# Expert weights as plain float32 and token slots in column tiles of 32, in a diffusion-step kernel

## What is computed

```python
def _expert_choice_ffn(h, router_w, wg, wu, wd):
    cap = EC_CAPACITY_FACTOR * n // N_EXPERTS            # 64 latent, 16 context slots
    probs = jax.nn.softmax((h @ router_w).astype(jnp.float32), axis=-1)
    gate, idx = lax.top_k(jnp.swapaxes(probs, 1, 2), cap)
    xs = h[b_idx, idx]
    hid = jax.nn.silu(jnp.einsum('becd,edf->becf', xs, wg)) * jnp.einsum('becd,edf->becf', xs, wu)
    ye = jnp.einsum('becf,efd->becd', hid, wd) * gate[..., None]
    return jnp.zeros_like(h).at[b_idx, idx].add(ye)
```

## Time and profile before

| | us |
|---|---|
| median of 3 runs | 1666.2 (1665.37 to 1667.24) |
| the profiled execution, its own time | 1663.94 |
| its span, first to last instruction | 1662.1 |
| PE's first and last expert matmul in it | 497.6 to 1627.4 |

### The profile page before, as it was taken

One profiled execution on the slowest core, in us unless ns is written; L12 is line 12 of the kernel. 1 busy time (PEld: TensorE's weight loads), 2 busy tenths in 40 slices (PEclk: granted clock), 3 DMA queues, 4 the chain that ended last, 5 costly groups with the idle time before them and its releaser, 6 DMA issues.

```text
span 1662.1 us, 18848 instructions
## 1 busy us (share of the span) xinstructions
PE 1504.0 (90%) x6785; PEld 1002.2 (60%) x6785; DVE 1207.9 (73%) x1072; ACT 964.2 (58%) x832; POOL 146.5 (9%) x80
## 2 busy tenths in 40 slices
PE   5798898669929999999999999999999999999991
PEld 2586676538806666666666666666666666666660
DVE  2536635332477888888888888889888888888883
ACT  3323444211416677776777777767767677767762
POOL 0422311200000000000000000000000000000000
PEclk9799999869859999999999999999999999999996
DMA  9321112481179999999999999999999999999953
GB/s 363 112 77 51 51 64 62 169 295 63 59 268 359 341 383 358 366 370 358 384 361 364 371 356 390 353 378 352 367 377 354 380 356 368 380 346 389 356 236 134
DMA packets 124210, 478.77 MB, mean 288 GB/s; under 512 B 11534, under 2 KB 13834, under 8 KB 107788
## 3 DMA queue, kind: packets, MB, share of 16 engines
q1 hardware_dynamic: 113796, 453.55, 73.0%
q0 software_dynamic: 3072, 10.49, 2.6%
q10 hardware_dynamic: 7304, 14.23, 2.4%
HBM read 464.59 MB, written 13.64 MB: 288 GB/s over the span
## 4 chain that ended last, share of the span: by engine, by line
PE 51%; DVE 21%; issue 12%; ACT 10%; DMA 5%; ACTq 0%; POOL 0%; DVEq 0%; SPq 0%; POOLq 0%
DVE w_lo L311 11%; PE bank L1047 8%; PE bank L1043 8%; PE bank L1044 8%; ACT w_hi L305 6%; PE bank L1061 4%; PE bank L1057 4%; PE bank L1058 4%; PE bank L346 3%; PE bank L348 3%; PE bank L347 3%; DMA raw<-in_ada_w 2%; PE bank L748 1%; PE bank L1070 1%; DVE arena L1456 1%
## 5 line engine op out<-in xcount | busy, mean ns | idle before, releaser
L311 DVE TENSOR_TENSOR w_lo<-raw,w_hi 128x2048 fp32r<-128x2048 f32 (+1 forms) x211 | 476.0, 2263 | 177.1 <-ACT w_hi L305 177.1
L305 ACT CAST w_hi<-raw 128x2048 fp32r<-128x2048 f32 x211 | 400.1, 1910 | 205.6 <-PE bank L1047 67.9
L311 DVE TENSOR_TENSOR w_lo<-arena,w_hi 128x2048 fp32r<-128x2048 f32 x189 | 427.0, 2285 | 52.4 <-ACT w_hi L305 52.4
L1043 PE MATMUL bank<-w_hi,act_lo 128*80 128x512 f32 x1024 | 406.5, 397 | 2.6 <-DVE act_lo L1462 2.3
L305 ACT CAST w_hi<-arena 128x2048 fp32r<-128x2048 f32 x189 | 357.9, 1910 | 80.7 <-PE bank L1047 79.7
L1044 PE MATMUL bank<-w_hi,act_hi 128*80 128x512 f32 x1024 | 402.6, 393 | 0.0
L1047 PE MATMUL bank<-w_lo,act_hi 128*80 128x512 f32 x1024 | 280.6, 396 | 3.7 <-DVE w_lo L311 3.7
L1043 PEld LDWEIGHTS bank<-w_hi,act_lo 128*80 128x80 f32 x1024 | 153.5, 150 | 90.0 <-ACT w_hi L305 6.9
L1047 PEld LDWEIGHTS bank<-w_lo,act_hi 128*80 128x80 f32 x1024 | 150.6, 148 | 94.1 <-DVE w_lo L311 10.8
L1057 PE MATMUL bank<-w_hi,act_lo 128*80 128x512 f32 x512 | 203.8, 398 | 0.0
L1058 PE MATMUL bank<-w_hi,act_hi 128*80 128x512 f32 x512 | 200.8, 392 | 0.0
(11 more groups left out here) (201 smaller groups left out, 1366.8 us busy)
## 6 DMA issues: line engine op xcount, KB each, us to landing
raw<-in_exp_up SPq DMA_DIRECT2D x66, 1024.0 KB, 6.8
raw<-in_exp_gate SPq DMA_DIRECT2D x65, 1024.0 KB, 8.7
raw<-in_exp_down SPq DMA_DIRECT2D x64, 1024.0 KB, 8.0
arena<-in_exp_down SPq DMA_DIRECT2D x64, 1024.0 KB, 6.9
arena<-in_exp_gate SPq DMA_DIRECT2D x63, 1024.0 KB, 8.8
arena<-in_exp_up SPq DMA_DIRECT2D x62, 1024.0 KB, 9.6
raw<-in_ada_w SPq DMA_DIRECT2D x24, 1024.0 KB, 9.2
raw<-in_w_in SPq DMA_DIRECT2D x12, 1024.0 KB, 7.0
```

The costliest lines, as they stand in the source:

```text
L305: nc.scalar.copy(w_hi[:, n % WS, :], landed(n)).then_inc(hi_done, 1)
L311: ops.tensor_tensor(w_lo[:, n % WS, at], landed(n)[:, at], w_hi[:, n % WS, at], ALU.subtract).then_inc(done, 1)
L1043: mm(dst, x[1][:, kk, :], wh[:, j, at], start=(kk == 0), stop=False)
```

## The change

Expert chunks are no longer rounded or split. PE takes them as landed, and the tokens are plain float32 too: `gathered` writes `xs` itself, `hidT_out` copies the turned hidden values once. Float32 matmuls have token tiles of 32 as the stationary operand: the 64 latent slots are two tiles, the 16 context slots a third, and four matmuls that follow each other write to the four different groups of 32 partitions of a bank. Gate and up chunks come in turn, a pair is used together (`gate_up`), and the order of `body_chunks` is by pairs. A ring slot is given back when PE has used the chunk (`x_used`), for a pair both at its end.

Silu and the product work on the new layout: latent gate in partitions 0 to 63 of banks 0 and 1, latent up in 64 to 127, both context parts in bank 2; two silus on 64 partitions and two on 16, and as many products, which take in the router's gate. At an expert's end ACT copies the latent half of the result from bank 4 and one half of the context result from bank 5, DVE adds the other half of it, so that `ye` waits for both engines. Ahead of the stage DVE has one memset and one small copy more, in the selection of the slots.

```diff
     def body_chunks(last):
+        def pair(b, nxt):
+            return [(kind, b, part, nxt) for part in range(4) for kind in "gu"]
+        def rows(b):
+            return [("d", b, half, 0) for half in range(2)]
         if last:
-            order = [("g", 1, 0), ("u", 1, 0), ("d", 0, 0), ("d", 1, 0), ("d", 2, 0), ("d", 3, 0)]
-        else:
-            order = [("g", 1, 0), ("d", 0, 0), ("d", 1, 0), ("u", 1, 0), ("g", 0, 1), ("d", 2, 0), ("d", 3, 0), ("u", 0, 1)]
+            return pair(1, 0) + rows(0) + rows(1) + rows(2) + rows(3)
+        return pair(1, 0) + rows(0) + rows(1) + pair(0, 1) + rows(2) + rows(3)
...
         else:
-            if i < N_EXP:
-                sp_e.wait_ge(lo_pool, i + 1)
-            sp_e.wait_ge(lo_dve, e * PER_E + (i + 1))
+            sp_e.wait_ge(x_used, e * PER_E + (i - N_EXP + 1))
...
-        def gathered_half(e, pr2, hf):
-            act.wait_ge(xs_f, 2 * e + (hf + 1))
-            nc.scalar.copy(xs[pr2][0][:, 4 * hf:4 * hf + 4, :], xs_tmp[:, hf, :].rearrange("p (k s) -> p k s", k=4)).then_inc(xs_h, 1)
...
+        def silu(n, e, own, p):
+            expert_used(act, n, e)
...
+            for b in range(2):
+                nc.scalar.activation(sgl[64:128, b, :], psum[b][0:64, :], ACT.Silu).then_inc(sl_ev, 1)
+                at = slice(32 * b, 32 * b + CAP_C)
+                nc.scalar.activation(sgl[at, 0, :], psum[2][64 + 32 * b:64 + 32 * b + CAP_C, :], ACT.Silu).then_inc(sl_ev, 1)
...
-                if not last or i + WS < len(chunks):
-                    split_hi(act, N_BODY + i + WS, e)
...
                     for hf in range(2):
-                        nc.scalar.activation(ye[0:SLOTS, hf * 512:(hf + 1) * 512], psum[4 + hf][0:SLOTS, :], ACT.Copy,
-                                             scale=gate[0:SLOTS, :]).then_inc(ye_rd, 1)
+                        at = slice(32 * hf, 32 * hf + CAP_C)
+                        nc.scalar.copy(sgl[at, 1, :], psum[5][64 + 32 * hf:64 + 32 * hf + CAP_C, :]).then_inc(yc_ev, 1)
+                    for hf in range(2):
+                        nc.scalar.copy(ye[0:CAP_L, hf * 512:(hf + 1) * 512], psum[4][64 * hf:64 * hf + 64, :]).then_inc(ye_rd, 1)
...
+        def gate_up(n, e, part, x):
+            g, u = expert_landed(pe, n, e), expert_landed(pe, n + 1, e)
+            for j in range(2):
+                kk = 2 * part + j
+                lat = [x[:, kk, 32 * i:32 * i + 32] for i in range(2)]
+                own = x[:, kk, CAP_L:SLOTS]
+                first, final = kk == 0, kk == 7
+                for b in range(2):
+                    c = slice(b * 512, (b + 1) * 512)
+                    for i in range(2):
+                        mm(psum[b][32 * i:32 * i + 32, :], lat[i], g[:, j, c], start=first, stop=final)
+                    for i in range(2):
+                        mm(psum[b][64 + 32 * i:96 + 32 * i, :], lat[i], u[:, j, c], start=first, stop=final)
+                for at, w in ((0, u), (64, g)):
+                    for b in range(2):
+                        last = mm(psum[2][at + 32 * b:at + 32 * b + CAP_C, :], own, w[:, j, b * 512:(b + 1) * 512],
+                                  start=first, stop=final)
+            last.then_inc(x_used, 2)
...
+            for j in range(2):
+                for hf in range(2):
+                    for i in range(2):
+                        mm(psum[4][64 * hf + 32 * i:64 * hf + 32 * i + 32, :], x[j][:, 32 * i:32 * i + 32],
+                           w[:, j, hf * 512:(hf + 1) * 512], start=first and j == 0, stop=final and j == 1)
+            for j in range(2):
+                for hf in range(2):
+                    at = 64 * j + 32 * hf
+                    last = mm(psum[5][at:at + CAP_C, :], x[j][:, CAP_L:SLOTS], w[:, j, hf * 512:(hf + 1) * 512],
+                              start=first, stop=final)
+            last.then_inc(x_used, 1)
...
-        def gathered_lo(e, pr2, hf):
...
-        def hidT_lo(e, b):
...
-        for n in range(N_EXP, N_EXP + WS):
-            split_lo(dve, "dve", n)
+        def hidden(e, own, p):
+            cp(gate[:, p:p + 1], gates[:, bass.ds(own, 1)]).then_inc(gate_rd, 1)
...
+            for b in range(2):
+                dve.wait_ge(sl_ev, 8 * own + (4 * p + 2 * b + 1))
+                stt(hid[0:CAP_L, b, :], psum[b][64:128, :], gate[64:128, p:p + 1], sgl[64:128, b, :], ALU.mult, ALU.mult)
...
+                    for hf in range(2):
+                        at = slice(32 * hf, 32 * hf + CAP_C)
+                        dve.wait_ge(yc_ev, 2 * e + (hf + 1))
+                        tt(ye[CAP_L:SLOTS, hf * 512:(hf + 1) * 512], psum[5][at, :], sgl[at, 1, :], ALU.add).then_inc(ye_rd, 1)
```

More of the change, by code:

```diff
@@ L100, in build @@
     rw = sb("rw", [P, KT, NEXP])
[L101 removed]
     slot_tok = sb("slot_tok", [P, NEXP], U32)
[L103 to L104 removed]
+    gates = sb("gates", [P, NEXP])
+    gate = sb("gate", [P, 2])
+    xs_t = sb("xs_t", [P, 2, KT * SLOTS])
     sm = sb("sm", [P, 128])
@@ L696, in body, with hidT_out @@
+        def hidT_out(e, b):
+            act.wait_ge(ht_ps, 4 * e + (b + 1))
+            nc.scalar.copy(hidT[:, b % 2, :], psum[(6, 3)[b % 2]][:, 0:4 * SLOTS]).then_inc(ht_ev, 1)
+        silu(N_EXP + 7, 0, 0, 0)
+        def body(e, pr2, last):
+            for i, (kind, b, part, nxt) in enumerate(body_chunks(last)):
                 turn = turn_after(last, kind, b, part)
                 if turn is not None:
-                    hidT_hi(e, turn)
-                if kind == "g" and part == 3:
-                    silu(N_BODY + i, e, 2 * b)
-                    silu(N_BODY + i, e, 2 * b + 1)
+                    hidT_out(e, turn)
+                if kind == "u" and part == 3:
+                    silu(N_BODY + i, e, e + nxt, b)
@@ new lines, in down @@
+        def down(n, e, b, half):
+            w = expert_landed(pe, n, e)
+            x = [hidT[:, b % 2, (2 * half + j) * SLOTS:(2 * half + j + 1) * SLOTS] for j in range(2)]
+            first, final = b == 0 and half == 0, b == 3 and half == 1
+            for j in range(2):
[9 more added lines that the diff above has]
+            last.then_inc(x_used, 1)
@@ L1076, in _ @@
         gather(0, 1)
-        pe.wait_ge(xs_l, 2)
+        pe.wait_ge(xs_f, 2)
         pe.wait_ge(ada_row, 12)
-        for i, (kind, b, part) in enumerate(FIRST_CHUNKS):
-            up_or_gate(N_EXP + i, 0, 2 if kind == "u" else 0, part, xs[0])
+        for part in range(4):
+            gate_up(N_EXP + 2 * part, 0, part, xs[0])
         def body(e, pr2, last):
@@ L1101, in body @@
                     if turn:
-                        pe.wait_ge(ht_lo, 4 * e + turn)
+                        pe.wait_ge(ht_ev, 4 * e + turn)
                     hid_T(e, turn)
-                if not last and i == 4:
+                if not last and i == 5:
                     gather(e + 1, 0)
-                if not last and i == 8:
+                if not last and i == 9:
                     pe.wait_ge(xs_f, 2 * e + 3)
@@ L1110, in body @@
                     pe.wait_ge(gbias2, 16)
-                    pe.wait_ge(sl_ev, 4 * NEXP)
                     pe.wait_ge(hid_rd, 4 * NEXP)
-                    gate_rows(rows, (0, 1, 2, 3))
-            pe.wait_ge(ye_rd, 2 * e + 2)
-        with pe.Fori(0, LAST - 1, 2) as e:
+                    gate_rows(rows, (0, 1, 2, 7))
+        body(0, 0, False)
+        body(1, 1, False)
+        with pe.Fori(2, LAST - 1, 2) as e:
             body(e, 0, False)
@@ L1488, in body @@
+        row_copy(11, 3, rows[:, 512:1024])
+        gathered(0, 0, 0)
+        gathered(0, 0, 1)
+        hidden(0, 0, 0)
         def body(e, pr2, last):
-            chunks = body_chunks(last)
-            for i, (kind, b, part, nxt) in enumerate(chunks):
+            for i, (kind, b, part, nxt) in enumerate(body_chunks(last)):
                 if not last and i in (5, 9):
-                    gathered(e + 1, i // 9)
-                    gathered_lo(e + 1, 1 - pr2, i // 9)
+                    gathered(e + 1, 1 - pr2, i // 9)
@@ L1494, in body @@
                 if kind == "u" and part == 3:
-                    hidden(N_BODY + i, e, e + nxt, 2 * b)
-                    hidden(N_BODY + i, e, e + nxt, 2 * b + 1)
-                if not last or i + WS < len(chunks):
-                    split_lo(dve, "dve", N_BODY + i + WS, e)
-                turn = turn_after(last, kind, b, part)
-                if turn is not None:
-                    hidT_lo(e, turn)
-                if kind == "u" and part == 3 and not nxt:
-                    cp(gate[0:SLOTS, :], slots[0:SLOTS, 1, bass.ds(e, 1)]).then_inc(gate_rd, 1)
+                    hidden(e, e + nxt, b)
@@ L1508, in _ @@
+        body(0, 0, False)
+        body(1, 1, False)
+        with dve.Fori(2, LAST - 1, 2) as e:
             body(e, 0, False)
```

188 lines of the change are left out of this document (69 added, 119 removed).

## The result

The changed kernel takes 1635.55 us in the median of four runs (1634.14 to 1637.11), the kernel before beside it 1666.27; the ratio is 0.9817, its 95% interval 0.9803 to 0.9831. That is 30.7 us faster. The forecast was 1600, some 66 us faster, with a range from 1558 to 1645. The profiled execution took 1634.74 us, its span is 1632.9.

The account below looks back on a forecast made before the run. PE's matmuls were taken to bound the expert stage. 493.6 + 2.6 + 990 + 38 + 19 + 3.4 + 8 + 5.5 = 1560; + 34.7 + 1.4 = 1596 span, so 1600 us; range 1558 to 1645.

Parts of the forecast that it names:

- Part 1: PE's expert matmuls: four narrow calls cost 0.86 us, a chunk 2.58 us in place of 2.77, 384 chunks 990 us.
- Part 2: Transposes interrupting PE's matmuls: 38 us as now, plus 0.2 us for each of 96 switches, 19 us (0 to 48).
- Part 3: Rounding and residuals leave ACT and DVE; 8 us left for PE's waits of the new order (0 to 24).
- Part 3's cover of silu and product: Expert stage: silus and products, some 3.5 us, hidden behind four down chunks of PE (10.3 us); uncovered, 112 us in all.
- Part 4: Ring slots held longer, SP waiting for PE: nothing charged in steady flow; cover gone if a landing takes over 13 us.
- The rival of late landings: Expert loop: PE stalls for landings once or twice an expert, 16 to 50 us, total 1615 to 1650; chance 0.16.
- Part 5: Stage start: first matmul at 493.6, 4 us gained; wait for loads 4 and 5 2.5 us, plus 3 (0 to 12).
- The 3 us for a thin ring: Stage start: 3 us added for the thinly filled ring behind PE's wait for loads 4 and 5.
- Part 6: End of the span: four ACT copies where two were, DVE adds behind them, 1.4 us more (0 to 3).
- The DMA at its limit: Expert weight loads: DMA already full at 356 to 375 GB/s, 1640 to 1695 us, most likely unchanged; chance 0.05.
- The groups that don't keep their step: PE's 1152 groups: at 0.93 us in place of 0.86, 81 us more, 1681 us; chance of slower 0.10.

Follow-up runs that it names:

- the two single edits: Changed kernel with the first pair of halves in banks 4, 5 and 3: 1628.65 us; changed kernel with the first eight loads in eight slots: 1627.01 us.
- the versions above: Follow-up kernels: changed kernel with PE's loop, first-pair banks or first loads altered, alone or together; 1589.29 to 1628.65 us.
- the fastest version: Changed kernel with one expert in a loop turn, first pair in banks 4, 5 and 3, first eight loads in eight slots: 1589.29 us.

## Why the prediction missed

The direction, the bound and the rate in steady flow were right; two costs were left out, one of them wholly, and the gain is less than half of the one forecast. The time lies inside the range of 1558 to 1645 by luck: its part above 1620 was made for late landings in the loop, and these did not come.

**Part 1 held.** The four calls of a group run side by side, and their instructions start in steps of 0.43 us at full clock: 1003.15, 1003.58, 1004.01 and 1004.44 are two groups. This stage's 0.86 us over 1152 groups speak for 4.0 times, as line 748 did. By the 3.07 times in the Trainium skill's page "TensorE: Matmul & The Clock Gate", Part 3, a group would take 1.12 us, an estimate; the trace does not agree.

**Part 2 was a little low.** Around the two kinds of transposes (L1078 of the hidden values, L1033 of the gathered rows), PE's timeline after:

```profile
1004.87 1.04 PE L1052 MATMUL bank<-arena,xs_t 128*16 128x512 f32 x8
1005.84 0.71 PE L1078 MATMUL bank<-const,arena 80*128 80x80 f32 x4
1006.48 0.62 PE L1047 MATMUL bank<-arena,xs_t 128*32 128x512 f32 x2
...
1016.72 1.04 PE L1052 MATMUL bank<-raw,xs_t 128*16 128x512 f32 x8
1017.69 0.49 PE L1033 MATMUL bank<-const,arena 80*128 80x80 f32 x4
1018.12 0.62 PE L1047 MATMUL bank<-raw,xs_t 128*32 128x512 f32 x2
```

The next group is due 0.86 us after 1004.87 and starts 1.61 after it, 0.75 late; at the gathered rows it is 1.40, 0.54 late. The forecast had 0.60 for each. Four sets of 0.75 and two of 0.54 are 4.1 us for an expert, and 24 chunks of 2.58 with them are 66.0: just what the beat shows.

**Part 3 is the step that failed, by what it did not list.** Its 8 us for waits of the new order are 0.5 us for each expert, and with the 65.5 of parts 1 and 2 they give the 66.0 seen, but by accident: no such waits exist, the transposes took it. What PE does wait for in the loop are the five jumps, 30.2 us with the slower clock behind them. The forecast counted PE's work in matmul time and its waits for other engines; getting PE's own instructions it put at nothing, without a reason. The counts for it stood in the windows: 442 matmuls and 441 weight loads in 100 us are 621 records in an expert of 70.3 us, 1240 in the turn of two; a float32 call is two instructions, so 288 calls in an expert become 576 matmuls with as many loads, with the transposes some 1200 (912 and 908 in the first 100 us above, 66 us for an expert), and 2400 in a turn of two. A turn of 1240 (before) and one of 1200 (one expert) ran without a stop, a turn of 2400 (after), one of 4800 (four experts) and one of 2480 (before, four experts) stopped at each jump. So by these counts, which leave out waits and branches, the limit lies between 1240 and 2400 records. The Trainium skill's page "Runtime: NRT & Kernel Launch", section "Instruction fetch mechanics", has a rule that would have pointed here: PE holds some 2048 instructions, they come in blocks of 16 KiB, and a taken branch to a block that isn't there stalls the engine. The traces agree on the block (1.69 MB in 103 packets, 16.4 KB each) and on the stall, and 2048 lies between the two counts above; the same section's other sentence, that the store is only two such blocks, is not what they show for PE, where a turn of 1240 stayed.

**Part 3's cover of silu and product** held in the loop: the wait for L1480 comes once in all, at 520 us. There the cover is missing, as the part's own condition says ("without that cover each pair of halves would cost 3.5 us"): the first pair has no down chunks behind it. The wait was 3.86 us, with its half clock 6.8. It was not seen that the first pair is such a place.

**Part 4 held.** SP waits for PE, 609.7 us for L1052 and 229.8 for L1069 in the stage, and PE never for a landing in the loop, though from 600 to 1500 us a landing took 10.0 us in the median and 14.6 at the longest, more than the 13 that the cover was put at. The rival of late landings came out near the measured time (1615 to 1650), but its mechanism is not there.

**Part 5 had the place, and its sum by luck.** First matmul at 491.95 where 493.6 was forecast; the gather of the first rows lands earlier as argued: PE waits 3.1 us for it where it waited 10.5. The stop for loads 4 and 5 came, at 504.2 for 4.2 us where 2.5 were forecast: PE went on 9.1 us after the first of the two loads was issued (499.27), not 7.4, which was worked out from the shortest landing. The 3 us for a thin ring did not come; the slower clock behind the stop, for which no allowance was made, did. Together the late loads cost 5.6 us against 5.5 charged. With the bank wait the start cost 12.4 us by the two single edits, just over the upper bound of 12.

**Part 6 held within its bounds.** The last matmul ends as ACT's copies begin, 36.8 us before the end of the span, where it was 34.7:

```profile
1596.11 1.18 ACT L708 COPY arena<-bank 16x512 f32<-16x512 f32 x2 [13.81 <-PE bank L1069]
```

That is 2.1 us more where 1.4 were forecast. 1.1 of it lies between the last matmul and the last scatter (1599.29), where the copies are. The other 0.9 lies behind the scatter, 33.6 us against 32.7, and the versions above have 31.7 to 33.6 there, so it can't be put down to the change.

**The balance.** 1596 forecast for the span, - 1.6 for the first matmul, + 6.9 at the start, + 30.2 at the jumps, + 0.7 at the end make 1632; the span is 1632.9. With both costs taken away the kernel takes 1589, 11 below the forecast: its start has no stop at all, where 5.5 us were charged, and its first expert matmul comes 3.8 us before the forecast's.

**The other rivals.** The DMA at its limit: it moves 385 and 391 GB/s in the windows without a stop, above the 356 and 375 of before, and 386 in the fastest version. The figure of about 358 GB/s in the Trainium skill's page "HBM Reference", section "Specifications (TRN2)", is passed over windows of 100 us; that section gives it as a core's share when both cores of a pair stream, and this kernel runs on one core. The groups that don't keep their step: not seen, apart from the few microseconds behind a stop.

## What to carry over

When an edit multiplies the instructions of an engine inside a hardware loop, count the instructions of one turn as well as their time: here a turn that was too long was fetched again, and each jump back stopped the engine for some 4 us with a wait that no semaphore explains; a shorter turn (one expert in place of two) or code written out took it away. Ask of every cover that a forecast counts on whether it is there in the first turn too. And price a stop of a busy TensorE with the slower clock behind it, here a third to three quarters more than the stop itself where the stop was near 4 us.

## What the runs showed of the hardware

- With the loop written out, PE's 22786 records (11393 matmuls and as many weight loads) go with 90 packets of 16.4 KB on the instruction queue, some 250 to a packet. Straight on, 4.7 packets in each 66 us are hidden entirely. At a jump back in a turn of 2400 or 4800 records PE stands 3.8 to 4.2 us; in one of 1200 it does not stand and no packet comes. Whether the stop would be shorter with idle DMA engines was not tried: weights were landing at 410 GB/s during it.
- A stop of 3.8 to 4.2 us in a stream at full clock was followed by 3 to 5.5 us at a granted clock of 0.50 to 0.58, even where PE had been full for 60 us ahead of it. Behind the first jump and behind 508.41 PE starts again at full clock and falls to half about a microsecond later; behind the stop at 520 and the other four jumps its first instructions already last 1.04 to 1.07 us, not 0.62. The stop of 2.81 us in the kernel before with four experts in a turn has full clock behind it (1.00 from 1241 to 1244 us).
- Groups of four narrow float32 calls in four different groups of 32 partitions, with 32 or 16 stationary columns, hold 0.43 us a step over 1100 us, so the 16-column calls of the context slots cost as much as the 32-column ones.
